# Two transformer blocks on one Trainium2 core: moving the FFNs' inner activations by 8 or 16 bytes in SBUF

## The reference, cut to what matters

```python
for layer in range(2):
    x = x + 0.5 * swiglu_ffn(rms_norm(x, ffn1_norm[layer]), ffn1_w_gu[layer], ffn1_w_down[layer])
    x = x + mixer(rms_norm(x, mix_norm[layer]))
    x = x + memory_cross_attention(...)
    x = x + 0.5 * swiglu_ffn(rms_norm(x, ffn2_norm[layer]), ffn2_w_gu[layer], ffn2_w_down[layer])
x = x + rms_norm_2(recurrent_and_sparse_attention_mixer(x), norm_mix_post)
f = (silu(h @ w_ffn_gate) * (h @ w_ffn_up)) @ w_ffn_down
x = x + rms_norm_2(f, norm_ffn_post)

def swiglu_ffn(x, w_gu, w_down):
    gate, up = jnp.split(x @ w_gu, 2, axis=-1)
    return (jax.nn.silu(gate) * up) @ w_down
```

## Time and profile before

| | |
|---|---|
| runs | 3130.27, 3130.39 and 3130.66 us, median 3130.39 us |
| profiled execution | span 3127.9 us from the first to the last instruction, 2.5 us under the median of the runs; its own time outside the span isn't given |
| TensorE (PE) busy | 3112.8 us, 100% of the span, 14504 matmul records |
| TensorE's weight loads (PEld) busy | 2517.6 us, 80% |
| VectorE (DVE), ScalarE (ACT), GpSimd (POOL) busy | 1581.5 us (51%), 1219.4 us (39%), 318.7 us (10%) |
| granted TensorE clock | 1.000 over the whole span |
| DMA | 290.95 MB, 93 GB/s on the average |

### The profile page before, as it was taken

How to read it: one execution, slowest core, us unless ns; L and a number is a source line. 1 busy time by engine, 2 the same in 40 slices (tenths; PEclk the granted TensorE clock), 3 DMA queues, 4 the chain that set the end, 5 groups by cost and what they waited for, 6 DMA issues and landing times. The chain is left out here.

```text
span 3127.9 us, 37166 instructions
## 1 busy us (share of the span) xinstructions
PE 3112.8 (100%) x14504; PEld 2517.6 (80%) x14504; DVE 1581.5 (51%) x2479; ACT 1219.4 (39%) x1994; POOL 318.7 (10%) x454
## 2 busy tenths in 40 slices
PE   9999999999999999999999999999999999999999
PEld 8888886878888888888866878888887786788887
DVE  5443358754444344433566754443346876564433
ACT  4332247543232233223455543322335727443222
POOL 1000114211000000001210200000142200020000
PEclk9999999999999999999999999999999999999999
DMA  5333331412332333333222413332232231223332
GB/s 159 94 95 101 96 94 35 148 61 88 101 101 95 95 95 94 101 98 97 89 95 82 148 48 101 95 101 95 86 101 81 77 108 33 84 86 95 99 97 74
DMA packets 214368, 290.95 MB, mean 93 GB/s; under 512 B 13072, under 2 KB 138384, under 8 KB 214064
## 3 DMA queue, kind: packets, MB, share of 16 engines
q1 hardware_dynamic: 211120, 279.26, 28.6%
q0 software_dynamic: 2496, 8.98, 0.9%
q10 hardware_dynamic: 576, 0.33, 0.0%
HBM read 286.42 MB, written 2.10 MB: 92 GB/s over the span
## 5 line engine op out<-in xcount | busy, mean ns | idle before, releaser
L103 DVE TENSOR_TENSOR wl<-raw,wh 128x1024 fp32r<-128x1024 f32 (+2 forms) x531 | 654.1, 1239 | 1068.2 <-ACT wh L100 1064.3
L100 ACT ACTIVATE wh<-raw 128x1024 fp32r<-128x1024 f32 (+2 forms) x531 | 552.1, 1048 | 1142.9 <-PE ps L94 1103.8
L94 PE MATMUL ps<-hTh,wh 128*128 128x512 f32 x2400 | 942.1, 393 | 0.7 <-ACT hTh L100 0.7
L94 PE MATMUL ps<-hTh,wl 128*128 128x512 f32 x2400 | 938.0, 391 | 0.0
L94 PE MATMUL ps<-hTl,wh 128*128 128x512 f32 x2400 | 895.6, 391 | 0.2 <-DVE hTl L109 0.2
L94 PEld LDWEIGHTS ps<-hTh,wh 128*128 128x128 f32 x2400 | 450.8, 188 | 101.8 <-issue 9.9
L94 PEld LDWEIGHTS ps<-hTh,wl 128*128 128x128 f32 x2400 | 450.8, 188 | 97.3 <-issue 7.1
L94 PEld LDWEIGHTS ps<-hTl,wh 128*128 128x128 f32 x2400 | 449.4, 188 | 96.9 <-issue 4.7
L103 POOL TENSOR_TENSOR xn<-xn 128x512 f32<-128x512 f32 x69 | 99.2, 1438 | 1769.1 <-ACT xn L100 1531.7
L94 PE MATMUL ps<-wh,hTh 128*128 128x512 f32 (+2 forms) x576 | 216.8, 377 | 0.0
L94 PE MATMUL ps<-wl,hTh 128*128 128x512 f32 (+2 forms) x576 | 215.1, 374 | 0.0
(11 more groups left out here) (418 smaller groups left out, 4005.2 us busy)
## 6 DMA issues: line engine op xcount, KB each, us to landing
raw<-in_ffn_w_gu SPq DMA_DIRECT2D x350, 256.0 KB, 3.1
raw<-in_ffn_w_down SPq DMA_DIRECT2D x88, 512.0 KB, 3.5
raw<-in_xa_w_kv SPq DMA_DIRECT2D x32, 512.0 KB, 3.9
raw<-in_w_in SPq DMA_DIRECT2D x28, 512.0 KB, 3.7
raw<-in_od_w_in SPq DMA_DIRECT2D x24, 512.0 KB, 3.6
raw<-in_w_ffn_gate SPq DMA_DIRECT2D x44, 256.0 KB, 2.8
raw<-in_w_ffn_up SPq DMA_DIRECT2D x44, 256.0 KB, 3.1
raw<-in_w_ffn_down SPq DMA_DIRECT2D x22, 512.0 KB, 3.8
```

The costliest lines, as they stand in the source:

```text
L94: return self.made(lambda e: e.matmul(*a, **k))
L100: return self.made(lambda e: e.activation(*a, **k))
L103: return self.made(lambda e: e.tensor_tensor(*a, **k))
```

## The change

`Ffn` gets a further argument, `skew`, in numbers of 4 bytes. Its two large tiles are no longer taken as [128, 22, 512] at 128 modulo 512. The new method `rows` moves the area's pointer to 32 bytes below such an address, takes a tile of 22 x 512 + 16 numbers there, and uses the 22 x 512 numbers that begin at number 8 + skew. With a skew of 0 they would begin at 128 modulo 512 again. With 4, -4, 2, -2 and 4 they begin 16 bytes after (f10), 16 before (f20), 8 after (f11), 8 before (f21) and 16 after it (f3). `Fh` of f10 goes from 126592 to 126608, and its `Fl` from 171648 to 172176; `sg`, `pr` and `R` come 1024 bytes later than before and keep 128 modulo 512. Nothing else moves: each engine has the same instructions in the same order with the same shapes, and the same waits.

```diff
     class Ffn:
-        def __init__(self, up, down, tag):
+        def __init__(self, up, down, tag, skew):
             area = Area(base)
             self.up, self.down = up, down
-            self.F = Act(sb(tag + "Fh", [P, KF, S], F32R, area), sb(tag + "Fl", [P, KF, S], F32R, area), S, ("F", up))
+            self.F = Act(self.rows(tag + "Fh", area, skew), self.rows(tag + "Fl", area, skew), S, ("F", up))
             self.sg = [sb(f"{tag}sg{i}", [P, S], F32, area) for i in range(2)]
             self.pr = [sb(f"{tag}pr{i}", [P, S], F32, area) for i in range(2)]
             self.R = sb(tag + "R", [P, S], F32, area)
 
-    ffns = {t: Ffn(u, d, t) for t, u, d in (("f10", "f1u0", "f1d0"), ("f20", "f2u0", "f2d0"), ("f11", "f1u1", "f1d1"),
-                                            ("f21", "f2u1", "f2d1"), ("f3", "f3u", "f3d"))}
+        def rows(self, name, area, skew):
+
+            area.at = in_step(area.at) - 32
+            t = area.take(nc, name, [P, KF * S + 16], F32R)
+            return t[:, 8 + skew:8 + skew + KF * S].rearrange("p (k s) -> p k s", k=KF)
+
+    ffns = {t: Ffn(u, d, t, k) for t, u, d, k in (("f10", "f1u0", "f1d0", 4), ("f20", "f2u0", "f2d0", -4),
+                                                  ("f11", "f1u1", "f1d1", 2), ("f21", "f2u1", "f2d1", -2),
+                                                  ("f3", "f3u", "f3d", 4))}
```

## The result

The changed kernel takes 3145.32 us (median of 4 runs, 3143.77 to 3146.11) against 3130.47 us before; the ratio is 1.0047, with a 95% interval of 1.0031 to 1.0062. That is 14.9 us or 0.47% slower.

A forecast was written before the change was run, and what follows sets the result against it. The prediction took TensorE's product count times the distance between starts as the bound. Its terms summed to 0 on the 3127.9 us span; adding 2.5 us to reach the median gave 3130.4 us, range 3116 to 3146 us.

The forecast's parts named there:

- What bounds the kernel: Whole kernel: TensorE, busy 3112.8 of 3127.9 us; time is the number of products times the distance between their starts.
- The term of 0 for the products: Five down projections: the 2640 products with a shifted operand stay at 226.7 ns each, adding 0 us.
- the prediction's own sign: Down projections: forecast is wrong if distances average over 2.4 ns off 226.7 across the five, or another stage's distance moves.
- the bounds: Price of the 2640 shifted products: -35.2 us if 13.3 ns each vanish, +35.2 us if each costs 13.3 ns more.
- the row after a break: Twelve distances after a break in the product sequence, 230.8 ns each: +4.1 ns, or +10.8 us over 2640 products.
- The writes of F at 0 to 2 ns each: ScalarE and VectorE writes of F in the up projection: 0 to 2 ns more each, hidden even at 100 ns.
- the row of `evQ`: Stick-breaking stage: VectorE reads a row 16 bytes past a multiple of 64 in 693 ns, against 691 ns aligned.
- `sg`, `pr` and `R` at nothing: Tiles placed 1024 bytes later at the same phase: no cost, since no engine's row depends on it.
- Steps of 13.3 ns: TensorE products: distances of 120.0, 133 and 226.7 ns are close to multiples of 13.3 ns, as if starts came in steps.
- Rival 1: Down projections: changed offset between the two reads prevents settling, 230.8 ns each, +10.8 us, 3141.2 us; chance 0.18.
- Rival 2: Down projections: starts off a line boundary cost 13.3 ns, +14.1 us in f11 and f21, 3144.5 us; chance 0.14.
- Rival 3: Down projections: offset parts the colliding reads, 213.3 ns at the least; -14.1 us for two FFNs, 3116.3 us; chance 0.18.

The follow-up runs named there:

- experiment 4: Kernel before the change with only the eight weight buffers `wh` and `wl` moved 32 bytes against all else: 3205.82 us against 3130.86 us, ratio 1.0239.
- experiment 5: Kernel before the change with every tile of whole rows, moving, stationary and other, moved by 32 bytes: 3130.63 us against 3130.86 us, ratio 0.9999.
- experiment 1: Changed kernel with all five offsets set to 0, padding and new places of `Fl`, `sg`, `pr`, `R` kept: 3130.96 us against 3130.53 us, ratio 1.0002.
- the sweep: Changed kernel cut down to a loop of 63 series of 72 fp32r products, varying starts and columns: 226.7 ns at no offset, 236.9 ns with moving operand 4 bytes off.
- the 224 and 150 series: Product loops alone: 224 pairs of starts, 226.7 to 240.0 ns; 150 series with separate offsets for high and low rows and weights, 226.7 to 237.8 ns.
- the grid: Product loop alone with 224 pairs of moving and stationary starts, 44 products each: 226.7 ns in 25 series, highest 240.0, mean 232.4 ns.

## Why the prediction was right or wrong

**What bounds the kernel: right.** The lengthening is all in the distance between fp32r products, 15.94 of 15.95 us, and in the 2640 products named.

**The term of 0 for the products: wrong, and this is the step that failed.** By the prediction's own sign (more than 2.4 ns off 226.7 on the average of the five) the forecast of no change is refuted. I took 0 because every moving read begins as far from the one before as it did, and because a weight load is short and hides. That only the offset between moving and stationary read is new was right, but it does count: 6.2 ns on each of 12,048 products where nothing but the weights moved (experiment 4), and 0 where both moved by 32 bytes (experiment 5). "It hides" was said of the weight loads' time: they are still busy for 99 of about 123 us and TensorE is never idle there, yet where they read from changes the distance. The term measured +16.0 us, 6.0 ns per product instead of 0; of the bounds, +10.8 us from the row after a break was the near one, and -35.2 and +35.2 us held it. That the time lies inside the stated range is luck in part: the upper end came from rivals 1 and 2, neither of which happened with its mechanism and its price, and the measured time is 0.7 us below it.

**The writes of F at 0 to 2 ns each, off the path: right** (633 to 634 and 691 to 689 ns, no new wait), and so was the row of `evQ` as their bound. **`sg`, `pr` and `R` at nothing: right** (experiment 1). One reading there was a little off: the last four rows of F are read bank by bank, so the first reader of the last row comes after 225 products, 51 us, and not 54; the cover is ample either way.

**Steps of 13.3 ns: wrong.** Three distances fitted, but the sweep found 125.2, 131.7, 216.7 and, by offsets, 228.9, 230.0, 231.7, 233.3, 236.7 and 240.0 ns. What repeats is a cycle of some products whose sum is a multiple of 6.67 ns.

**Rival 1, the loss of the settled state: the right kind, with the wrong size.** It named the relation of the two reads, and its threshold of three FFNs was passed by all five. But 230.8 ns is no state of its own. It is the mean of twelve distances between 225 and 236 ns, of which the last three are back at 226 and 227 ns: a short way in to the settled state. The changed products don't stay in it; they settle in other cycles, mostly at 233.3 ns. Priced at +4.1 ns each it gave 3141.2 us; at the measured 6.0 ns it gives 3146 us.

**Rival 2, the boundary: fell.** 16 bytes cost 5.0 or 6.7 ns and 8 bytes 6.7, 128 bytes about as much, and 28 and 60 bytes nothing. The Trainium skill, SBUF — State Buffer, section "Specifications (TRN2)", has 16-byte lines with a penalty for each crossing; by that rule offsets of 16 and 128 bytes would be free, and those of 28 and 60 bytes, which end within a line, would cost. The runs show +5.0 to +6.7 ns for the first and 0 for the second, so the rule doesn't describe what happened here.

**Rival 3, faster: fell.** None of the 224 and 150 series, and none of the first sweep's with 512 fp32r columns, is below 226.7 ns. The 215.7 ns of the Trainium skill, TensorE: Matmul & The Clock Gate, section "Wait — 56ns, not 53.3ns?", is met by bf16 (215.8 ns) and not by fp32r. The 11 ns between the two are real, but no start address that was tried wins them back.

**How a surer forecast could have been had.** The rows after the break already said that equal shapes at equal phases don't always follow each other at 226.7 ns. That a settled state exists which can be lost, and that no row of before has another offset, was a reason to give the slower side more than 0.32: of the 224 series of the grid 25 keep 226.7 ns, about one in nine.

**Open.** Why the relation of the two starts counts, the rule behind the grid (why 28 and 60 bytes are free and 32 isn't), and what picks one of two states weren't settled. That the spread of the changed kernel's runs (3143.77 to 3146.11 us) comes from f3's two states was not tested.

## What to carry to other kernels

Where a stream of full-rate fp32r products bounds a kernel, keep all operands of such products at one phase, high and low parts alike: here equal phases at a common shift of 0, 32, 64, 128 or 256 bytes, and differences of 256, 512 and 1024 bytes at no shift, held the lowest distance each time. Read such a loss from the distance of product starts; the waits show nothing, and the busy share was 100% before and after. And when a trace has only one value of a quantity that a change varies, a short series of products by itself can answer in one run what no row of before can; test the answer in the kernel, since one pair of starts settled in two ways.

## What the runs showed of the hardware that was not expected

- The distance of fp32r products of 512 columns depends on the start addresses of both operands in steps of 4 bytes, from 226.7 to 240.0 ns; bf16 (215.8 ns) and fp32 (two records of 429.2 ns) showed no dependence at five starts of the moving operand.
- The settled state at 226.7 ns is locked to a common time grid. In the kernel before, the 39 longest stretches at 226.7 ns, with breaks of any length between them, all start on one grid of 6.67 ns that drifts only slowly against the timestamps: the remainder goes from 2.3 ns at 19 us over 0.0 at 1500 us to 4.3 ns (that is, -2.3) at 3035 us.
- The same starts can have two states: f3's products in the changed kernel run at 226.7 ns in some stretches and at 233.3 ns in others, and 16 bytes on both operands gave 233.4 ns in one sweep and 230.0 ns in another.
